# In the scan, GpSimd's two products move behind VectorE's decay work, and the next decay transfer is issued ahead of them

## The reference, cut to what matters

```
x_dt = (xh * dt[..., None])
a_cs = jnp.cumsum(da, axis=-1)
seg = a_cs[..., :, None] - a_cs[..., None, :]
lmat = jnp.exp(jnp.where(causal, seg, -jnp.inf))
y_diag = jnp.einsum("bgrcls,bcsgrp->bclgrp", cb[:, :, None] * lmat, x_dt)
decay_states = jnp.exp(a_cs[..., -1:] - a_cs)
states = jnp.einsum("bclgn,bgrcl,bclgrp->bcgrpn", bc, decay_states, x_dt)
...
y = (y + d_skip[i][None, None, :, None] * xh)
```

## Time and profile before

| | us |
|---|---|
| median of 3 runs | 1279.6 |
| lowest, highest | 1279.49, 1281.93 |
| the profiled execution, own time | 1278.81 |
| its span | 1277.1 |
| PE busy in the span | 1186.4 (93%) |
| DVE busy | 492.3 (39%) |
| POOL busy | 195.3 (15%) |

### The profile page before, as it was taken

The page is one execution under the profiler, slowest core; times in us unless marked ns, Lnnn a source line. Parts: engine busy times, 40 slices in busy tenths (PEclk is TensorE's granted clock), DMA queues, the critical chain, the costliest instruction groups (busy, mean ns, idle before and its releaser), DMA issues. The chain is left out here.

```text
span 1277.1 us, 13414 instructions
## 1 busy us (share of the span) xinstructions
PE 1186.4 (93%) x4799; PEld 610.8 (48%) x4799; DVE 492.3 (39%) x1007; ACT 245.7 (19%) x611; POOL 195.3 (15%) x320
## 2 busy tenths in 40 slices
PE   4999999998999999999999999999999998978886
PEld 2535865466554444448954444444444343423332
DVE  5676035655646412112775223223222222212247
ACT  2141122224432100000121212212111111111111
POOL 5000021111002000001261121221111121211100
PEclk9999999999999999999999999999999999989998
DMA  9742232124358943229057999999999999999966
GB/s 302 196 132 66 67 133 86 63 83 133 100 161 285 415 180 111 66 72 364 35 218 272 308 413 421 423 423 423 418 406 407 407 397 402 396 391 391 401 253 261
DMA packets 110985, 334.66 MB, mean 262 GB/s; under 512 B 14356, under 2 KB 67688, under 8 KB 83912
## 3 DMA queue, kind: packets, MB, share of 16 engines
q1 hardware_dynamic: 87824, 269.37, 55.1%
q0 software_dynamic: 18400, 47.10, 10.5%
q10 hardware_dynamic: 4696, 17.35, 3.3%
HBM read 314.49 MB, written 38.35 MB: 276 GB/s over the span
## 5 line engine op out<-in xcount | busy, mean ns | idle before, releaser
L1860 PE MATMUL ps<-gu_hi,xsT 128*64 128x512 f32 (+1 forms) x704 | 244.8, 621 | 27.2 <-DMA gu_hi<-in_exp_w_up_dram 11.9
L1860 PE MATMUL ps<-gu_lo,xsT 128*64 128x512 f32 (+1 forms) x320 | 147.3, 615 | 10.1 <-issue 6.4
L1860 PEld LDWEIGHTS ps<-gu_hi,xsT 128*64 128x64 f32 (+1 forms) x704 | 85.0, 156 | 138.6 <-issue 136.9
L1362 DVE SCALAR_TENSOR_TENSOR hid<-ps,wgt,gated 128x256 f32<-128x256 f32 x42 | 20.3, 484 | 307.2 <-ACT gated L940 307.2
L1868 PE MATMUL ps<-dn_hi,hidT 128*64 128x512 f32 (+1 forms) x352 | 119.9, 597 | 1.1 <-DVE hn L1358 1.1
L1507 PE MATMUL ps<-n1T,ring 128*128 128x512 f32 x256 | 111.9, 594 | 0.0
L1737 PE MATMUL ps<-n1T,ring 128*128 128x512 f32 x256 | 110.9, 593 | 0.7 <-ACT attT L880 0.7
L705 POOL DMA_INDIRECT expert_rows<-hn,meta x40 | 39.9, 998 | 395.1 <-DVE hn L1358 353.3
L1358 DVE TENSOR_TENSOR hn<-ps,g_row 128x1024 f32<-128x1024 f32 x42 | 51.4, 1225 | 91.7 <-PE ps L1868 91.5
L1860 PEld LDWEIGHTS ps<-gu_lo,xsT 128*64 128x64 f32 (+1 forms) x320 | 51.4, 166 | 61.9 <-issue 61.7
L940 ACT ACTIVATE gated<-ps 128x256 f32<-128x256 f32 x42 | 16.1, 383 | 333.6 <-PE ps L1860 333.6
(11 more groups left out here) (336 smaller groups left out, 1350.4 us busy)
## 6 DMA issues: line engine op xcount, KB each, us to landing
gu_hi<-in_exp_w_gate_dram SPq DMA_DIRECT2D x44, 1024.0 KB, 16.3
gu_hi<-in_exp_w_up_dram SPq DMA_DIRECT2D x44, 1024.0 KB, 30.5
dn_hi<-in_exp_w_down_dram SPq DMA_DIRECT2D x44, 1024.0 KB, 29.3
ring<-in_w_in_dram SPq DMA_DIRECT2D x21, 1024.0 KB, 5.5
gu_lo<-in_exp_w_gate_dram SPq DMA_DIRECT2D x20, 1024.0 KB, 15.7
gu_lo<-in_exp_w_up_dram SPq DMA_DIRECT2D x20, 1024.0 KB, 30.8
dn_lo<-in_exp_w_down_dram SPq DMA_DIRECT2D x20, 1024.0 KB, 30.9
h<-in_ada_w_dram POOLq DMA_DIRECT2D x32, 512.0 KB, 5.4
```

The lines of the kernel that those rows point to most:

```text
L1860: ins = pe.matmul(ps[rows, 2 + b, :], xsT[:, b, k, rows], gu(s)[:, :, k, :], start=(k == 0), stop=(k == KC - 1))
```

## The change

In GpSimd's loop over the tiles three things are changed. `spread(t + 1)` now stands first. A wait for `m_done` to reach 2t + 2, that is for both of DVE's multiplications of tile t, stands behind it. And `xdec` is formed ahead of `skip`, both behind that wait; in tile 3, where there is neither a next transfer nor an `xdec`, `skip` alone stands behind it. No instruction with data is added or removed, and no other engine's code changes.

```
@@ -599,8 +599,9 @@
             for t in range(T):
                 if t >= 1:
                     pool.wait_ge(y_read, t)
-                pool.wait_ge(xtok_done, t + 1)
-                pool.tensor_tensor(heads(skip), heads(u[:, t, :]), over(dskip, HD), ALU.mult).then_inc(skip_done, 1)
+                if t < T - 1:
+                    spread(t + 1)
+                pool.wait_ge(m_done, 2 * t + 2)
                 if t < T - 1:
                     if t >= 1:
                         pool.wait_ge(y_ready, t)
@@ -608,7 +609,8 @@
                     pool.wait_ge(ex_done, t + 1)
                     pool.tensor_tensor(heads(xdec), heads(xdt), over(ex[:, HEADS:2 * HEADS], HD),
                                        ALU.mult).then_inc(xdec_done, 1)
-                    spread(t + 1)
+                pool.wait_ge(xtok_done, t + 1)
+                pool.tensor_tensor(heads(skip), heads(u[:, t, :]), over(dskip, HD), ALU.mult).then_inc(skip_done, 1)
                 pool.wait_ge(mean_done, T + t + 1)
                 pool.tensor_tensor(urs[:, :], urs[:, :], mhalf[:, 0:GROUPS], ALU.pow).then_inc(root_done, 1)
```

## The result

The changed kernel takes 1268.12 us (median of 4 runs, 1267.13 to 1269.08) against 1279.88 us (4 runs, 1279.49 to 1281.93): 11.8 us less, a ratio of 0.991 with a 95% interval of 0.9898 to 0.9922. The forecast was 1268.7 us. The profiled execution took 1268.09 us with a span of 1266.3 us, 10.8 us under the span before.

A forecast was written before the change was run, and what follows sets the result against it. The scan was taken as bound by DVE, whose clamping GpSimd's products delay, then by TensorE. Tile gains 0 + 4.58 + 4.60 + 1.67 = 10.85 us took 1279.6 to 1268.7 us; range 1266.8 to 1273.2 us.

The forecast's parts named there:

- What bound the scan: Tiles 1 to 3: TensorE idles 3.08, 3.08 and 1.91 us for DVE's late multiplications; afterwards TensorE is the bound.
- The price of a product over the clamping: DVE's 16 clamping instructions: each GpSimd product over them costs 1.67 us; undisturbed, the 16 take 3.19 us.
- its list of signs: What the changed profile should show, such as 0.2 us of TensorE idle time in tile 3.
- Line 1613 at the upper clock: TensorE, tiles 1 and 2: without idle time the line takes 2.02 us instead of 3.59, about 1.5 us gained.
- The products' new place is covered: GpSimd behind the multiplications: at 1.90 us each, both products end 0.8 us before they are wanted in tile 1.
- The bound for two products at 2.87 us: Both GpSimd products late in their new place: the gain would be 8.5 us instead of 10.9.
- The transfer first, worth nothing: GpSimd's decay transfer, issued ahead of the products: data wanted over 20 us later, so nothing gained or lost.
- The rival that GpSimd is held by it: GpSimd waits 5.2 us for its transfer's landing: gain only 6.8 us, 1272.8 us; chance 0.07.
- The slower rival: GpSimd held far longer after its transfer, at 10.4 us: 5.8 us slower, 1285.4 us; chance 0.03.
- The sum: Gains over tiles 0 to 3 of the scan: 0 + 4.58 + 4.60 + 1.67 = 10.85 us.
- That it is handed on whole: Stages behind the scan start from its semaphores and move as a block, so the whole 10.85 us reaches the end.
- The size of the whole: Whole kernel: 10.9 us off the median of 1279.6 us, giving 1268.7 us.

The follow-up runs named there:

- warm: The kernel before, with three extra TensorE matmuls (results written over) in the idle time of tiles 1 and 2; 1277.6 us.
- transfer_last: The changed kernel with the next decay transfer put back behind the two products, which still wait for m_done; 1269.6 us.
- as_changed: The changed kernel, unaltered, timed again against the kernel before; 1268.7 us.
- held: The changed kernel with GpSimd made to wait until its just-issued decay transfer has landed before forming the two products; 1274.9 us.
- fill_over: The changed kernel with one more GpSimd instruction, a memset of the skip area, over DVE's clamping; 1269.8 us.
- skip_gated: Against the kernel before, only skip is moved behind m_done; xdec is formed early, over DVE's clamping; 1272.0 us.
- seg_gate: As transfer_last, but the two products wait for seg_done (clamping over) instead of m_done (multiplications over); 1273.8 us.
- skip_first: The changed kernel with the two products exchanged, skip then xdec, both behind m_done; 1270.3 us.
- xdec_gated: Against the kernel before, only xdec is moved behind m_done; skip stands where it stood, over the clamping; 1273.8 us.

## Why the prediction was right

- **What bound the scan** (VectorE before line 1613, TensorE behind it): right. With VectorE free, the idle time went and nothing else became late; line 1088 is still released by TensorE.
- **The price of a product over the clamping**, 1.67 us: measured 6.53 - 4.87 = 1.66 and 4.87 - 3.22 = 1.65 us. The undisturbed 16 take 3.22 us, predicted 3.19. In tile 3 TensorE idles 0.27 us; the prediction's working gives 0.1 us, and its list of signs says 0.2.
- **Line 1613 at the upper clock**: right, 2.05 us from start to start against the 2.02 taken from tile 0, and shown apart by warm.
- **The products' new place is covered**: right. Of the two prices offered for a product, 1.90 and 2.87 us, the row that started free was the one to take. The cover was 1.0 us by the timeline, 0.8 in the prediction, since a product starts within 0.1 us of its releaser and not 0.3 (which was a transfer's issue; that lags its releaser by 0.53 to 0.94 us here).
- **A slip that cost nothing.** The bound for two products at 2.87 us, a gain of 8.5 us, charges VectorE's whole lateness of 1.1 us in tiles 1 and 2, although the prediction itself forgives 0.9 us of it before `turn_u`. With that counted the gain would be an estimated 10.3 us. The products took 1.9 us, so neither figure was tried.
- **The transfer first, worth nothing**: right, by transfer_last. The rival that GpSimd is held by it fell: `xdec` begins 1.28 us after the issue ended, released by VectorE. The slower rival fell with it.
- **The sum**: 10.85 us predicted, 10.92 measured in the scan stretch: 0.00, 4.64, 4.65 and 1.63 us in tiles 0 to 3, where 0, 4.58, 4.60 and 1.67 were forecast. That it is handed on whole holds as well: from the first attention products to the span's end the kernel before took 1277.1 - 305.38 = 971.7 us, the changed one 1266.3 - 294.05 = 972.3 us.
- **The size of the whole**: that it comes so close is in part luck, for there was a term that the prediction did not have, the clock behind the last wait in tile 3. In the profile of before line 1633 takes 1.97 us there, in the changed kernel's it takes 1.16 us, both behind 3.17 us of idleness:

```profile
300.26 1.97 PE L1633 MATMUL ps<-ident,h 128*128 128x128 f32 x8 [3.17 <-DVE h L1104]
...
305.38 2.90 PE L1664 MATMUL ps<-kdup,raw 64*64 64x64 f32 x64 [0.91 <-issue]
```
```profile
294.05 2.90 PE L1666 MATMUL ps<-kdup,raw 64*64 64x64 f32 x64 [0.91 <-issue]
```

From tile 3's product with the state to the first attention products the two profiles take 15.45 and 14.12 us. In as_changed, which is the same program as the changed kernel, this takes 15.55 us, and in warm, which is the kernel before but for its extra matmuls, 14.13. So it falls one way or the other from run to run, and nothing ties it to the change. The spans differ by 10.8 us because these 1.33 us were about cancelled: in the changed profile the scan began 0.92 us later (177.99 us; 177.48 in as_changed), and the stages behind it took 0.53 us more. The first comparison of medians gave 11.8 us and the second 10.8 us; by what was set down ahead of the second, that makes the excess scatter between runs. Whether it was this clock is not shown.

## What to carry to other kernels

When one or two of a row of equal instructions on VectorE take seven times as long as the rest, lay GpSimd's timeline over them: here each GpSimd instruction cost VectorE one wait of about its own length. GpSimd work belongs where VectorE is waiting for a third engine, gated by VectorE's last instruction that must be on time and with the product that is wanted first in front. An idle stretch of TensorE costs its length and can cost more in clock for the small matmuls behind it: here 1.3 to 1.5 us behind 3.08 us of idleness, and nothing behind 1.42 or 1.91 us. Closing a long one can so be worth more than the wait that the profile shows.

## What the runs showed of the hardware

- Beside a memset of 0.96 us on GpSimd, which reads nothing, a VectorE `tensor_scalar` lasted 1.06 us; beside a product, which takes 1.90 us when undisturbed, one lasted 1.93 us. Undisturbed ones last 0.27 to 0.29 us. Two-input products of the two engines took turns: 2.85 us for 1.22 us of work on VectorE, 2.76 and 2.88 us for 1.90 on GpSimd.
- Behind the same 3.17 us of idleness TensorE's next eight transposes took 1.16 us in some executions (changed, transfer_last, held, fill_over, skip_gated, warm) and 1.97 us at a granted clock of 0.50 in others (before, as_changed, seg_gate, skip_first; in xdec_gated behind 3.23 us). Behind two stretches of 1.45 and 1.41 us with 1.2 us of work between, the granted clock was down twice out of two (0.67 and 0.63), and behind the single ones of 1.42 us in skip_gated and xdec_gated it was 1.00. In held it was 1.00 behind 2.20 us and 0.70 behind 2.40 us.
